# Two chained transformer blocks on one core: keys of the second attention from split fp32r operands, computed after the values

## The reference

```python
proj = h @ w_in
xr, q, ckv, qi, ki, wi, gr, ga = jnp.split(proj, split_points, axis=-1)
y_rnn = rg_lru(causal_conv(xr, conv_w, conv_b), ...)
ckv = rmsnorm(ckv, kv_norm_g)                 # 256 x 512
...
# per head: keys = ckv @ w_uk (512 x 128), values = ckv @ w_uv, top-64 positions by an index score
logits = q_lat . c_sel * 128 ** -0.5;  p = softmax(logits);  o = (p c_sel) w_uv
mixed = sigmoid(gr) * y_rnn + sigmoid(ga) * y_attn      # 16 heads of 128
x = x + mixed @ w_o;  x = x + peer(rmsnorm(x), ...)
```

## Time and profile before

| what | value |
|---|---|
| median of 3 runs | 2716.55 us (2716.38 to 2718.21) |
| the profiled execution's own time | 2715.33 us |
| its span in the trace | 2713.5 us |
| PE busy | 2689.9 us, 99% |
| DVE, ACT, POOL busy | 1879.4 (69%), 1383.0 (51%), 357.0 us (13%) |
| TensorE clock granted over the span | 0.999 of full speed |
| matmuls of keys (L2387) and values (L2392) | first 803.5 us, last 1052 us |

### The profile page before, as it was taken

One profiled execution on the slowest core, in us unless ns is written; L12 is line 12 of the kernel. 1 busy time (PEld: TensorE's weight loads), 2 busy tenths in 40 slices (PEclk: granted clock), 3 DMA queues, 4 the chain that ended last, 5 costly groups with the idle time before them and its releaser, 6 DMA issues.

```text
span 2713.5 us, 48127 instructions
## 1 busy us (share of the span) xinstructions
PE 2689.9 (99%) x14366; PEld 2315.8 (85%) x14366; DVE 1879.4 (69%) x3046; ACT 1383.0 (51%) x2114; POOL 357.0 (13%) x422
## 2 busy tenths in 40 slices
PE   8999999999999999999999999999999999999998
PEld 7888888898888888888888888888888888888887
DVE  6666665658986666489897888886665555555555
ACT  6454545556655444455465555554544444444444
POOL 0000000000001110011105666660000000000000
PEclk9999999999999999999999999999999999999999
DMA  7545455555555545655566556556666666656564
GB/s 258 192 158 172 162 192 186 174 207 169 168 176 167 162 155 160 193 192 190 197 208 200 192 196 196 194 197 207 213 212 217 217 216 218 211 193 193 194 239 156
DMA packets 162488, 522.19 MB, mean 192 GB/s; under 512 B 18048, under 2 KB 42880, under 8 KB 161408
## 3 DMA queue, kind: packets, MB, share of 16 engines
q1 hardware_dynamic: 131472, 478.35, 54.4%
q10 hardware_dynamic: 30960, 43.14, 4.5%
HBM read 504.63 MB, written 16.78 MB: 192 GB/s over the span
## 4 chain that ended last, share of the span: by engine, by line
PE 94%; DVE 3%; ACT 1%; issue 1%; DMA 0%; SPq 0%; DVEq 0%; ACTq 0%
PE bank L540 31%; PE bank L547 16%; PE bank L2589 8%; PE bank L2591 8%; PE bank L2590 8%; PE bank L580 5%; PE bank L581 4%; PE bank L582 4%; PE bank L2558 1%; PE bank L2392 1%; PE bank L2387 1%; DVE w_lo L483 1%; PE bank L506 1%; PE bank L507 1%; PE bank L508 1%
## 5 line engine op out<-in xcount | busy, mean ns | idle before, releaser
L483 DVE TENSOR_TENSOR w_lo<-raw,w_hi 128x1024 fp32r<-128x1024 f32 x902 | 1095.6, 1224 | 690.1 <-ACT w_hi L474 683.9
L474 ACT ACTIVATE w_hi<-raw 128x1024 fp32r<-128x1024 f32 x902 | 952.2, 1060 | 937.6 <-PE bank L547 354.2
L540 PE MATMUL bank<-act,w_hi 128*128 128x512 f32 x3840 | 975.6, 396 | 2.0 <-DVE big L1433 0.8
L540 PEld LDWEIGHTS bank<-act,w_hi 128*128 128x128 f32 x3840 | 692.1, 189 | 133.1 <-issue 5.6
L547 PEld LDWEIGHTS bank<-act,w_lo 128*128 128x128 f32 x3840 | 519.9, 190 | 33.1
L547 PE MATMUL bank<-act,w_lo 128*128 128x256 f32 x3840 | 535.7, 282 | 0.0
L2589 PE MATMUL bank<-w_hi,expert_act 128*128 128x512 f32 x1008 | 392.4, 389 | 0.4 <-DVE cst L558 0.4
L2590 PE MATMUL bank<-w_lo,expert_act 128*128 128x512 f32 x1008 | 392.2, 389 | 0.0
L2591 PE MATMUL bank<-w_hi,expert_act 128*128 128x512 f32 x1008 | 392.2, 389 | 0.0
L686 POOL TENSOR_SCALAR hot<-cst,stat 128x128 fp32r<-128x128 f32 x256 | 255.1, 1010 | 129.1 <-PE bank L2558 128.8
L2589 PEld LDWEIGHTS bank<-w_hi,expert_act 128*128 128x128 f32 x1008 | 189.2, 188 | 40.0 <-DVE cst L558 0.8
(11 more groups left out here) (330 smaller groups left out, 2462.9 us busy)
## 6 DMA issues: line engine op xcount, KB each, us to landing
raw<-in_stream SPq DMA_DIRECT2D x902, 512.0 KB, 4.1
z_kept<-cst ACTq DMA_DIRECT2D x96, 128.0 KB, 2.2
cst<-z_kept ACTq DMA_DIRECT2D x96, 128.0 KB, 3.9
big<-in_ukv ACTq DMA_DIRECT2D x16, 512.0 KB, 4.6
big<-in_rows ACTq DMA_DIRECT2D x3, 1024.0 KB, 5.6
big<-in_x SPq DMA_DIRECT2D x2, 1024.0 KB, 9.4
big<-in_rg_w ACTq DMA_DIRECT2D x1, 2048.0 KB, 9.3
x_kept<-big ACTq DMA_DIRECT2D x1, 2048.0 KB, 7.4
```

The source lines that it names most:

```text
L474: act.activation(w_hi[:, s, :], raw[:, s, :], ACT.Copy).then_inc(hi_ready, 1)
L483: dve.tensor_tensor(w_lo[:, s, :], raw[:, s, :], w_hi[:, s, :].bitcast(F32), ALU.subtract).then_inc(lo_ready, 1)
L540: pe.matmul(bank[:, :], w_hi[:, s, kk * P:(kk + 1) * P], act2[:, k, :, :].rearrange("p a n -> p (a n)"), start=(k == 0), stop=False)
```

## The change

The keys' fp32 product becomes three fp32r products. `CKVT` is split once: `ckvt_hi` by ACT right after `CKVT` is copied out (128 x 1024), `ckvt_lo` by POOL (128 x 1024) as the first thing it does for the recurrence, once the index sums are final. The key half of `UKV` (128 x 512) is split per head: `uk_hi` by ACT, `uk_lo` by POOL. `keys_values` makes the values first, then the keys. `ckvt_lo` lies where `ISC` and the old `AMASK` lay, so `AMASK` moves to the columns of `KID` and `KIT`; `uk_hi` and `uk_lo` lie inside `RGW`, so head 0's split waits until block 14's gate weights are staged and runs in an unrolled last turn of the recurrence. Two semaphores that nobody waited for are dropped.

```diff
+        with nc.sbuf_tensor("below_uk", [P, 11008], F32), \
+                nc.sbuf_tensor("uk_hi", [P, RT, P], F32R) as uk_hi, \
+                nc.sbuf_tensor("uk_lo", [P, RT, P], F32R) as uk_lo:
+            pass
...
-        AMASK = at(31232, TT * S)
+        AMASK = at(32000, TT * S)
...
 (POOL)
+            def split_uk_lo(h):
+                pool.wait_ge(uk_hi_ready, h + 1)
+                pool.tensor_tensor(uk_lo[:, :, :], UKV[:, 0:RT, :], uk_hi[:, :, :].bitcast(F32), ALU.subtract)\
+                    .then_inc(key_lo_ready, 1)
+
+            pool.wait_ge(ckvt_kept, RT + 1)
+            pool.wait_ge(rel_used, 2 * IH + TT + 1)
+            pool.tensor_tensor(ckvt_lo[:, :, :], CKVT, ckvt_hi[:, :, :].bitcast(F32), ALU.subtract)\
+                .then_inc(key_lo_ready, 1)
             with pool.Fori(0, KT) as j:
...
+            split_uk_lo(0)
             wait_summed(pool, block_of("rnn", KT - 1, 2, 1))
...
                     pool.tensor_tensor(gate_rows, gate_rows, RSTD_ROW, ALU.mult).then_inc(scaled, 1)
+                    if not n and not last:
+                        split_uk_lo(h + 1)
...
 (ACT)
+            act.wait_ge(ckvt_kept, RT)
+            act.activation(ckvt_hi[:, :, :], CKVT, ACT.Copy).then_inc(ckvt_kept, 1)
+
+            def split_uk_hi(h):
+                act.wait_ge(ukv_ready, h * 16 + 16)
+                act.wait_ge(k_made, h)
+                act.activation(uk_hi[:, :, :], UKV[:, 0:RT, :], ACT.Copy).then_inc(uk_hi_ready, 1)
...
-            with act.Fori(1, KT) as j:
+            with act.Fori(1, KT - 1) as j:
                 rnn_block(j)
+            act.wait_ge(ukv_ready, 16)
+            act.wait_ge(w_staged, KT - 1)
+            act.activation(uk_hi[:, :, :], UKV[:, 0:RT, :], ACT.Copy).then_inc(uk_hi_ready, 1)
+            rnn_block(KT - 1)
...
                 if first:
-
+                    split_uk_hi(h + 1)
                     act.wait_ge(rw_ready, 1)
                     act.activation(RW, RW, ACT.Sqrt, scale=0.25).then_inc(rw_root, 1)
...
                 act.activation(TG, TG, ACT.Tanh, scale=0.5).then_inc(gr_tanh, 1)
+                if not first and not last:
+                    split_uk_hi(h + 1)
...
 (PE, keys_values)
                 pe.wait_ge(ukv_ready, h * 16 + 16)
-                pe.wait_ge(ckvt_kept, RT)
-                pe.wait_ge(k_kept, h + 1)
-                for k in range(RT):
-                    ins = pe.matmul(banks[2][:, 0:S], UKV[:, k, :], CKVT[:, k, :], start=(k == 0), stop=(k == RT - 1))
-                ins.then_inc(k_made, 1)
+                pe.wait_ge(ckvt_kept, RT + 1)
                 pe.wait_ge(v_kept, h + 1)
                 for st in range(2):
                     for k in range(RT):
                         ins = pe.matmul(banks[3][:, st * P:(st + 1) * P], CKVT[:, k, st * P:(st + 1) * P],
                                         UKV[:, RT + k, :], start=(k == 0), stop=(k == RT - 1))
                 ins.then_inc(v_made, 1)
+                pe.wait_ge(key_lo_ready, h + 2)
+                pe.wait_ge(k_kept, h + 1)
+                for k in range(RT):
+                    pe.matmul(banks[2][:, 0:S], uk_hi[:, k, :], ckvt_hi[:, k, :], start=(k == 0), stop=False)
+                    pe.matmul(banks[2][:, 0:S], uk_hi[:, k, :], ckvt_lo[:, k, :], start=False, stop=False)
+                    ins = pe.matmul(banks[2][:, 0:S], uk_lo[:, k, :], ckvt_hi[:, k, :], start=False, stop=(k == RT - 1))
+                ins.then_inc(k_made, 1)
```

More of the change, by code:

```diff
@@ L160, in build @@
         gate_in_lo = gate_act[:, :, 1, :]
+        with nc.sbuf_tensor("below_uk", [P, 11008], F32), \
+                nc.sbuf_tensor("uk_hi", [P, RT, P], F32R) as uk_hi, \
+                nc.sbuf_tensor("uk_lo", [P, RT, P], F32R) as uk_lo:
+            pass
+        with nc.sbuf_tensor("below_ckvt_lo", [P, 30720], F32), \
+                nc.sbuf_tensor("ckvt_lo", [P, RT, S], F32R) as ckvt_lo:
+            pass
         big = sb("big", [P, NB * S])
+        with nc.sbuf_tensor("ckvt_hi", [P, RT, S], F32R) as ckvt_hi:
+            pass
         with nc.sbuf_tensor("expert_act", [P, 2, 2, S], F32R) as expert_act:
@@ L328, in build @@
         ukv_ready = sem("ukv_ready")
+        uk_hi_ready = sem("uk_hi_ready")
+        key_lo_ready = sem("key_lo_ready")
         xf_ready = sem("xf_ready")
@@ L369, in build @@
         scored = sem("scored")
-        sc_masked = sem("sc_masked")
         sc_max = sem("sc_max")
@@ L417, in build @@
         logits_made = sem("logits_made")
-        logits_masked = sem("logits_masked")
         max_ready = sem("max_ready")
@@ L657, in _, with scale_head @@
                 pool.tensor_copy(WST, RGW[:, bass.ds(j, 1), :].rearrange("p o n -> p (o n)")).then_inc(w_staged, 1)
+            split_uk_lo(0)
             wait_summed(pool, block_of("rnn", KT - 1, 2, 1))
-            with pool.Fori(0, H2) as h:
+            def scale_head(h, last=False):
                 pool.wait_ge(logits_made, h + 1)
@@ L665, in _ @@
                     pool.tensor_tensor(gate_rows, gate_rows, RSTD_ROW, ALU.mult).then_inc(scaled, 1)
+                    if not n and not last:
+                        split_uk_lo(h + 1)
+            with pool.Fori(0, H2 - 1) as h:
+                scale_head(h)
+            scale_head(H2 - 1, last=True)
             def add_copied(dest, halves, block):
@@ L1698, in _ @@
             for t in range(TT):
-                step(dve.tensor_tensor(IWORK[:, t, :], ISC[:, t, :], c("causal")[:, t * S:(t + 1) * S], ALU.add))
+                dve.tensor_tensor(IWORK[:, t, :], ISC[:, t, :], c("causal")[:, t * S:(t + 1) * S], ALU.add)\
+                   .then_inc(rel_used, 1)
+            dve.wait_ge(rel_used, 2 * IH + TT + 1)
             def next_eight():
```

## The result

| | before | after |
|---|---|---|
| median of 5 runs of each | 2716.38 us (2715.78 to 2718.21) | 2741.23 us (2739.96 to 2742.77) |
| the profiled execution's own time, its span | 2715.33, 2713.5 us | 2742.22, 2740.4 us |

The ratio is 1.0093, 95% interval 1.0081 to 1.0104: the change makes the kernel slower by 24.9 us, at the forecast's 2739.8 within 1.4 us. Lines have moved: the first split is L483, the low half L492, the gate products L549 and L556, the copy of the values L1844, the scaling of the probabilities L1873, the values' matmuls L2429, the keys' L2435 to L2437, the transposes L2482.

What follows compares the result with a forecast made beforehand. PE was taken to bound the kernel, busy 2689.9 of 2713.5 us. Recurrence 0.7, head 0 2.8 and heads 19.7 sum to +23.2 us on 2715.33; with the median 1.2 above that execution, 2739.8 us, range 2724 to 2750.

Steps and rivals of the forecast that it cites:

- The keys: In each head, twelve fp32r matmuls take 1.44 us for the four fp32 ones' 1.73: 0.29 us saved, 4.6 in 16 heads.
- The order: With values in front of keys, PE waits for DVE's copy L1803 to free bank 3: 0.68 us a head.
- POOL and DVE shut each other out: In heads 1 to 14, uk_lo holds DVE's L1832, so L1803 comes 1.02 us later: +1.41 us a head, 19.7 in all.
- POOL's length: uk_lo on POOL in the loop over heads: 1.23 us, interpolated between rows of 256 and 1024 columns.
- the second rival: POOL is slower into fp32r: uk_lo takes 2.41 us, ckvt_lo 4.8; +42.1 us, 2758.7. Chance 0.10.
- Start of the recurrence: ckvt_lo on POOL holds DVE's split, so PE's query product at 628.91 waits: +0.7 us, bounds 0.3 to 1.5.
- Head 0: uk_hi of head 1 stands ahead of the square root, waits for its load and delays PE's values: +2.8 us.
- the landing: In head 0, the load that uk_hi waits for lands in 3.5 to 4.8 us, mostly 4.6.
- My list of rivals: Unheld copy 2725.6 us (0.22); slow POOL 2758.7 (0.10); values' bank free 2712.6 (0.07); faster by over 0.2% (0.02).
- a falling clock in the heads: Sign of being wrong: a granted clock that falls in the heads, which none of the cases has.
- the 19.7 us of the heads: PE's wait of 1.70 us at the values, less 0.29 saved on keys: +1.41 us a head in 14 heads.
- the not-slower one: v_kept is posted before PE enters the pair, so all 16 heads keep 0.29 us: -3.9 us, 2712.6. Chance 0.07.

Runs made afterwards that it cites:

- E5: Changed kernel with DVE's copy of the values moved ahead, right behind the maximum of the logits and ahead of finish_head: 2715.68 us, ratio 0.9999.
- E1: Kernel before with only the order changed, values ahead of keys, both still fp32 and nothing split: 2727.36 us, ratio 1.0042.
- E3: Changed kernel with POOL's uk_lo of heads 1 to 14 waiting until DVE has posted the copy of the values: 2725.91 us, ratio 1.0039.
- E6: Changed kernel with ckvt_lo on POOL only after block 11 of the recurrence: 2739.16 us, ratio 1.0084.
- the first repeat: Changed kernel run once more, unchanged, to see whether the granted clock falls in head 0 again: 2740.66 us.
- E4: Changed kernel with uk_hi of head 1 put behind the square root in head 0: 2739.84 us, ratio 1.0089.
- E2: Changed kernel with the keys put back in front of the values: 2729.29 us, ratio 1.005.
- E7: Changed kernel with the edits of E4, E5 and E6 together: 2714.01 us, ratio 0.9994.
- E9: Changed kernel with three more turns of ACT's recurrence loop written out, the same work in a longer program: 2741.06 us.
- the two repeats: Changed kernel run twice more, unchanged, for the granted clock in head 0: 2740.66 and 2741.51 us.

## Why the prediction was right, by its own steps

**The keys.** Forecast 0.29 us saved a head, measured 0.30 (E5). The sum is right, in part by luck: the twelve matmuls take 1.51 us (1.52 in E5) and not 1.44, and the values, now in front, take 1.71 in E5 where they took 1.78 (886.99 to the transposes at 888.77). The prediction had left the values' price alone.

**The order.** Forecast a wait of 0.68 us; measured +0.73 a head with nothing else changed (E1), and a standstill of 0.67 in E3.

**POOL and DVE shut each other out.** Forecast: L1803 1.02 us later, PE's wait 1.70, +1.41 a head. Measured: 0.98 by E3, 1.66 in the row of the weight loads, +1.41. The Trainium skill, "SBUF — State Buffer", in its section on SBUF's two sides, says of the shared pair that the one that starts first keeps it for its whole length. The trace agrees at this size too: 1.54 us for 0.55 behind a POOL instruction that started 0.08 ahead. In all 14 heads where the two meet it was the first scaling that stood behind POOL, by some 0.09 us: it took 1.28 us for 0.29, the second its 0.34 as before. The other order, POOL between the two scalings, never came up.

**POOL's length.** Interpolated 1.23 us, measured 1.28 to 1.30. This is the row of all sixteen:

```profile
L662 POOL TENSOR_TENSOR uk_lo<-big,uk_hi x16: 1278/1280/1298, 800.5 to 1070.6; 128x512 fp32r<-128x512 f32 x16
```

It refutes the second rival: into fp32r POOL writes no slower than into fp32. The estimate from the Trainium skill's "GPSIMD Engine Reference", 1.12 us, was 0.16 too low. `ckvt_lo` took 2.40 us, the forecast 2.41:

```profile
620.94 2.40 POOL L667 TENSOR_TENSOR ckvt_lo<-big,ckvt_hi 128x1024 fp32r<-128x1024 f32 x1 [321.70 <-DVE big L1738]
621.37 3.05 DVE L492 TENSOR_TENSOR w_lo<-raw,w_hi 128x1024 fp32r<-128x1024 f32 x1
623.30 1.62 POOL L672 TENSOR_TENSOR big<-big 128x256 f32<-128x256 f32 x1
...
629.71 2.10 PE L549 MATMUL bank<-act,w_hi 128*128 128x512 f32 x8 [0.46 <-DVE big L567]
```

**Start of the recurrence.** Forecast +0.7 us at PE's product of 628.91. It starts 0.81 us later, and E6 takes just that away.

**Head 0.** The chain ran as forecast: landing, split, table load, root, copy, PE.

```profile
812.77 0.35 ACTq L1036 DMA_DIRECT2D big<-in_ukv  x1
...
816.19 0.64 ACT L971 ACTIVATE uk_hi<-big 128x512 fp32r<-128x512 f32 x1 [0.18 <-DMA big<-in_ukv]
...
818.14 3.63 ACT L1045 ACTIVATE big<-big 128x4096 f32<-128x4096 f32 x1
...
822.37 2.98 PE L2429 MATMUL bank<-big 128*128 128x128 f32 x16 [1.95 <-DVE big L1844]
```

The term that was mis-sized is the landing. I took 4.6 us, the median; from issue to the split's start it is 3.4, below the 3.5 that I had given as the lower bound. From the first pair to the second PE took 16.22 us before and takes 18.22 after, 2.0 more; the forecast's 822.72 makes it 3.07. This is 1.1 us too much.

**What the sum lacked.** In the first repeat, without a clock fall in head 0, the last pair starts 22.46 us later than before and is 0.3 shorter: +22.2 at the end of the heads, the forecast's 23.2 less the landing. The span is 25.4 longer, so 3.2 us more come behind the heads. These are the late turn: PE's wait grows by 1.6 (0.20 to 1.83), and the clock falls behind it, for 1.6. My list of rivals had no case for either, and I had written that a falling clock in the heads would speak against all of them. It fell, and the mechanism stands: two misses, 3.2 us too little (4.8 where the clock falls in head 0) and 1.1 too much, partly cancel. That the median came within 1.4 us is therefore partly luck; the 19.7 us of the heads are not (in that repeat 1.41 in 13 turns and 1.31 in the other, 19.6 in all).

**The rivals.** The values' bank found free, the not-slower one, needs DVE's copy 0.62 us earlier against PE. E5 does just that and takes away 25.6 us, so the rival was right in its price of the heads and wrong only in that the change doesn't do it.

## What to carry to other kernels

A product that is followed by another often hides the release of the other's bank. Before you turn two around, read in the timeline how late the releaser of the second is: here 0.68 us a head, more than twice what the cheaper keys saved.

An instruction put on an idle engine is only free if its ports are. `uk_lo` on an idle POOL delayed a DVE pair of 0.55 us by 1.0, because it started 0.08 us ahead of it; one semaphore to hold it back was worth 15.3 us (13.7 of them in the heads), and moving the waited-for copy out from behind the pair 25.6.

Where both are mended the edit is worth at most what it saves on the bounding engine, 0.3 us a head, 4.8 in all, and a side effect elsewhere can take that.

## What the runs showed of the hardware that I had not expected

**The clock falls after short waits, but not each time.** Behind PE's wait of 1.7 to 1.9 us at the late turn the granted clock fell to 0.5 for some 3 us in six of ten profiles (the changed kernel's three, E4, E5, E6) and stayed at 1.00 in four (E2, E3, E7, E9), with waits of 1.77 to 1.89 and of 1.74 to 1.86. Behind the wait of 1.8 to 2.0 us in head 0 it fell in two of six (the first profile after, E9) and not in the two repeats, E3 and E6. Behind the fourteen waits of about 1.5 us in the heads it never fell, nor behind E4's one wait of 1.80 us in head 1. So at these two places the wait had a second price, some 1.6 us, and in head 0 it came and went between executions of one kernel. The clock does not explain the spread of the runs by itself: the changed kernel's spread over 2.8 us, but the five runs of the kernel before, which has neither wait, over 2.4.

**A stall far from the edit.** ACT's 1.65 us more between two DMA issues some 790 us behind the last edited instruction came with every kernel that had the split keys, and with no other. It is neither the length of ACT's program nor the time of the turn. It is a DMA store that lands 1.6 us later, its last eight packets starting only when a load of program is done; with the split that load starts earlier against the store, and why is open.
